# A decoder layer on one Trainium2 core: the router and the end go by token tile, and one unit of expert weights gets a twelfth place

## What is computed

```python
h = rms_norm(x, norm_mix)
z = h @ w_in                                  # queries, keys, values, gates of both branches
oa = moba_attention(qa, ka, va) @ w_oa        # branch A
ob = dsa_attention(qb, kb, vb, ...) @ w_ob    # branch B: indexer, top 64, low-rank keys and values
x = x + (sigmoid(ga) * oa + sigmoid(gb) * ob) @ w_out
x = x + cross_attention(rms_norm(x, norm_x), rms_norm(mem, mem_norm), wq, wk, wv, wo)
# mixture of experts: 4 groups of 8, the best group, in it the best 2 of 8
h = rms_norm(x, norm_moe)
g_logits, e_logits = h @ w_group + b_group, h @ w_router + b_router
weight = max(softmax(g_logits)) * softmax(top2(e_logits in the chosen group))
x = x + sum over the 2 chosen e of weight_e * (silu(h @ w1[e]) * (h @ w3[e])) @ w2[e]
return rms_norm(x, final_norm)
```

## Time and profile before

| | |
|---|---|
| time, median of 3 runs | 702.37 us (700.45 to 703.0) |
| the profiled execution: its own time | 700.77 us |
| its span | 699.0 us |
| mean granted clock | 0.883 |
| PE busy | 514.8 us, 74% |
| DVE busy | 201.8 us, 29% |
| ACT busy | 145.8 us, 21% |
| POOL busy | 15.7 us, 2% |
| DMA moved | 244.21 MB, 349 GB/s on the mean |
| the chain that ended last | PE 51%, DMA 43%, DVE 2%, ACT 2% |

### The profile page before, as it was taken

The page is one execution under the profiler, slowest core; times in us unless marked ns, Lnnn a source line. Parts: engine busy times, 40 slices in busy tenths (PEclk is TensorE's granted clock), DMA queues, the critical chain, the costliest instruction groups (busy, mean ns, idle before and its releaser), DMA issues.

```text
span 699.0 us, 8763 instructions
## 1 busy us (share of the span) xinstructions
PE 514.8 (74%) x3815; PEld 324.6 (46%) x3815; DVE 201.8 (29%) x368; ACT 145.8 (21%) x250; POOL 15.7 (2%) x28
## 2 busy tenths in 40 slices
PE   6999999999999987964735855582475577448284
PEld 5899998989998652411311321140131123114021
DVE  4699565595856430100100000010010000001002
ACT  6555545353644431000000000000000000000002
POOL 1200010001001000000000000000000000000001
PEclk9999999999999998988977797797798779779767
DMA  9899233615689889999999999999999999999991
GB/s 295 251 356 373 101 121 123 240 55 189 217 331 384 348 330 418 432 422 431 427 429 428 428 428 426 429 426 429 427 429 428 426 429 426 429 427 428 418 378 67
DMA packets 48089, 244.21 MB, mean 349 GB/s; under 512 B 8936, under 2 KB 18352, under 8 KB 37296
## 3 DMA queue, kind: packets, MB, share of 16 engines
q1 hardware_dynamic: 48048, 243.62, 86.3%
HBM read 242.53 MB, written 4.22 MB: 353 GB/s over the span
## 4 chain that ended last, share of the span: by engine, by line
PE 51%; DMA 43%; DVE 2%; ACT 2%; issue 1%; SPq 0%; POOL 0%; POOLq 0%; PEldq 0%; DVEq 0%; ACTq 0%
PE ps L640 16%; DMA slots_own<-in_w 13%; DMA slots_late<-in_w 12%; PE ps L934 11%; PE ps L939 7%; PE ps L659 7%; DMA slot_last<-in_w 5%; DMA slot_spare<-in_w 4%; DMA attn_data<-in_w 4%; DMA slot_mixed<-in_w 4%; PE ps L618 2%; PE ps L685 1%; PE ps L761 1%; DMA const<-in_consts 1%; PE ps L948 1%
## 5 line engine op out<-in xcount | busy, mean ns | idle before, releaser
L934 PE MATMUL ps<-slots_late,x_sb 128*32 128x512 f32 x336 | 86.8, 678 | 39.6 <-DMA slot_mixed<-in_w 15.8
L934 PE MATMUL ps<-attn_data,x_sb 128*32 128x512 f32 x176 | 71.5, 698 | 23.2 <-DMA slots_own<-in_w 23.2
L1585 DVE TENSOR_TENSOR bqT<-ps,bqT 128x512 f32<-128x512 f32 x8 | 5.5, 691 | 236.2 <-ACT bqT L1247 236.2
L939 PE MATMUL ps<-slots_own,vb 128*32 128x512 f32 x192 | 54.6, 736 | 24.8 <-DMA slot_last<-in_w 8.6
L410 DVE TENSOR_TENSOR w_low<-slots_own,w_high 128x2048 fp32r<-128x2048 f32 (+1 forms) x32 | 64.8, 2026 | 22.1 <-ACT w_high L1062 22.0
L1244 ACT ACTIVATE vb<-ps 128x256 f32<-128x256 f32 x8 | 3.1, 384 | 309.6 <-PE ps L976 309.6
L934 PE MATMUL ps<-slot_spare,x_sb 128*32 128x512 f32 x112 | 51.9, 668 | 14.1 <-DMA attn_data<-in_w 14.1
L934 PE MATMUL ps<-slots_own,x_sb 128*32 128x512 f32 x240 | 56.2, 674 | 6.9 <-DMA slots_late<-in_w 4.0
L1062 ACT ACTIVATE w_high<-slots_own 128x2048 fp32r<-128x2048 f32 (+1 forms) x32 | 54.3, 1695 | 20.2 <-PE ps L659 10.8
L640 PE MATMUL ps<-h_high,w_high 128*128 128x256 f32 x224 | 55.4, 288 | 0.0
L934 PEld LDWEIGHTS ps<-slots_late,x_sb 128*32 128x32 f32 x336 | 22.0, 123 | 71.0 <-issue 71.0
(11 more groups left out here) (263 smaller groups left out, 930.5 us busy)
## 6 DMA issues: line engine op xcount, KB each, us to landing
slots_own<-in_w SPq DMA_DIRECT2D x27, 2048.0 KB, 33.8
slots_late<-in_w SPq DMA_DIRECT2D x26, 2048.0 KB, 35.2
attn_data<-in_w SPq DMA_DIRECT2D x17, 2048.0 KB, 34.2
slot_last<-in_w SPq DMA_DIRECT2D x9, 2048.0 KB, 36.4
slot_spare<-in_w SPq DMA_DIRECT2D x9, 2048.0 KB, 33.8
slots_own<-in_w_in SPq DMA_DIRECT2D x8, 2048.0 KB, 11.7
slot_mixed<-in_w SPq DMA_DIRECT2D x8, 2048.0 KB, 32.5
slots_own<-in_w_out SPq DMA_DIRECT2D x2, 2048.0 KB, 7.9
```

The source lines that it names most:

```text
L934: return pe.matmul(ps[SLOTS * e:SLOTS * e + SLOTS, 4 + matrix, :], xeT[:, k, SLOTS * e:SLOTS * e + SLOTS], w, start=(k == 0), stop=(k == K ...
L939: return pe.matmul(ps[SLOTS * e:SLOTS * e + SLOTS, 4 + c, :], actT[:, f, SLOTS * e:SLOTS * e + SLOTS], w, start=(f == 0), stop=(f == FC - ...
L1585: dve.tensor_tensor(act_sb, ps[:, 5, :].rearrange("p (q f) -> p f q", f=FC), silu_sb.rearrange("p (f q) -> p f q", f=FC), ALU.mult).then_i ...
```

## The change

It has four parts.

- **A twelfth place.** B's gates `gb`, queries `bqT` and values `vb` become views of one buffer, `slot_extra`, of the size of a place. Unit 3 (`EXTRA_UNIT`) is loaded there, once, issued as the second of all units (`EXTRA_ASKED`), after the last reads of the three tensors. The other units keep the ring of eleven and its order (`ring_place`).
- **Other buffers.** Cross-attention's turned probabilities move from `gb` to `xn`, the router's scratch `rt` from `gb` to `memory_kv_data`, and the final gains from `memory_kv_data` to `slot_extra`; their load now stands after all units on SP.
- **The router.** `route` takes the tokens as the loaded operand and writes 128 x 36 logits straight away. The turning back, with ACT's two copies, is gone. Three of the four `start_sum` matmuls stand ahead of the ranking. DVE makes the places and the first `sel` before it computes the experts' weights (`finish_routing`), and the count goes to bank 7, to be read by the middle of the first gather.
- **The end.** The last sums are done tile by tile; ACT squares tile 0 after its two matmuls and tile 1 after all four. DVE multiplies by scale and gains in one op per half tile (L1625), and SP writes four pieces. The matmul of one element is now only in the branch that is not taken.

```diff
+EXTRA_UNIT = 3
+EXTRA_ASKED = 1
...
+def ring_place(q):
+
+    return q - 1 if q > EXTRA_UNIT else q
...
-        gb = sb("gb", [P, KD, T])
+        slot_extra = sb("slot_extra", [P, SLOT])
+        gb = slot_extra[:, 0:2048].rearrange("p (a b) -> p a b", a=KD)
...
-        bqT = sb("bqT", [P, 4, T])
-        vb = sb("vb", [P, TT, W_HEADS])
+        bqT = slot_extra[:, 2048:3072].rearrange("p (a b) -> p a b", a=4)
+        vb = slot_extra[:, 3072:4096].rearrange("p (a b) -> p a b", a=TT)
...
-        xprobT = flat(gb[:]).rearrange("p (h m t) -> p h m t", h=X_HEADS, m=2)
...
-        fgain = memory_kv_data[:]
+        xprobT = flat(xn[:]).rearrange("p (h m t) -> p h m t", h=X_HEADS, m=2)
+        rt = memory_kv_data[:, 0:14 * TT * EXPERTS].rearrange("p (n t e) -> p n t e", n=14, t=TT)
+        fgain = flat(gb)[:, 0:D]
...
-            for q in range(MOE_RING):
-                s = MOE_SLOTS[q]
+            for i in range(MOE_RING):
+                s = MOE_SLOTS[i]
+                if i == EXTRA_ASKED:
+                    sp.wait_ge(s_done, 8)
+                    sp.wait_ge(o_done, 8)
+                    sp.wait_ge(merge_added, 4)
+                    load_slice(EXTRA_UNIT % 2, 0, EXTRA_UNIT // 2, SLICE, slot_extra, extra_in)
...
+                load(i if i < EXTRA_UNIT else i + 1)
+            for q in range(MOE_RING + 1, ALL_UNITS):
+                i = ring_place(q) - MOE_RING
+                sp.wait_ge(chunk_used, (i if i < EXTRA_UNIT else i + 1) + 1)
                 load(q)
-            job_computed(sp, "xo3")
             sp.dma_start(fgain, final_norm.rearrange("(a d) -> a d", a=1).to_broadcast([P, D])).then_inc(fgain_in, 16)
-            for q in range(MOE_RING, ALL_UNITS):
-                sp.wait_ge(chunk_used, q - MOE_RING + 1)
-                load(q)
...
-                    m = pe.matmul(ps[0:N_RT, 6 + t, 0:P], w_rt[:, k, :], xT[:, k, t * P:(t + 1) * P],
+                    m = pe.matmul(ps[:, 6 + t, P:P + N_RT], xT[:, k, t * P:(t + 1) * P], w_rt[:, k, :],
                                   start=(k == 0), stop=(k == KD - 1))
-                m.then_inc(logitsT_done, 1)
+                m.then_inc(logits_done, 1)
...
+            start_sum(0, 0)
+            start_sum(0, 1)
+            start_sum(1, 0)
...
                 for k in range(KD):
+                    if slices_in and k == 4:
+                        pe.wait_ge(count_read, 1)
...
-                for c in range(2):
-                    pe.wait_ge((y_copied_a, y_copied_v)[c], it + 2)
-                    for t in range(TT):
+                for t in range(TT):
+                    for c in range(2):
+                        pe.wait_ge((y_copied_a, y_copied_v)[c], it + 2)
                         m = pe.matmul(ps[:, 2 * t + c, :], selwT[:, t * P:(t + 1) * P], y_sb[:, 512 * c:512 * c + 512],
                                       start=False, stop=True, skip_group_check=True)
+                    if t == 0 and slices_out:
+                        m.then_inc(top_done, 1)
...
-            act.wait_ge(logitsT_done, 1)
-            act.activation(rlT[:, 0:P], ps[0:N_RT, 6, 0:P], ACT.Copy).then_inc(logitsT_copied, 1)
-            act.wait_ge(logitsT_done, 2)
-            act.activation(rlT[:, P:T], ps[0:N_RT, 7, 0:P], ACT.Copy).then_inc(logitsT_copied, 1)
...
+            for t in range(TT):
+                act.wait_ge((top_done, added)[t], (1, STEPS + 1)[t])
+                square(ps[:, 2 * t:2 * t + 2, :], 5, t, xn[:, t, :].rearrange("p (a b) -> p a b", a=2), fsq)
...
+            for t in range(TT):
+                dve.wait_ge(frstd_set, t + 1)
+                for c in range(2):
+                    dve.scalar_tensor_tensor(xn[:, t, 512 * c:512 * c + 512], ps[:, 2 * t + c, :], rstd[:, 5, t:t + 1],
+                                             fgain[:, 512 * c:512 * c + 512], ALU.mult, ALU.mult).then_inc(out_set[t], 1)
```

128 lines of the change are left out of this document (57 added, 71 removed).

## The result

The changed kernel took **691.65 us** (median of 4 runs, 690.24 to 692.49) where the kernel before took 702.44 beside it (4 runs, 700.45 to 703.0): a ratio of 0.9852, 95% interval 0.9837 to 0.9867. Run again on another occasion it took 691.43 against 701.26, ratio 0.9855 (0.9839 to 0.9872). So it is 10.4 us faster by the ratio; 9.2 were forecast.

The account below looks back on a forecast made before the run. The expert weight stream was taken as the bound, 4.92 us a unit, with TensorE idling before landings. Place 4.9, router 1.8 and tail 2.5 sum to 9.2 us off the 702.37 median: 693.2 us, range 690 to 698.

Parts of the forecast that it names:

- The twelfth place: Early weight stream: unit 3's extra load fills holes, stream one unit ahead for good; gain 4.9 us, bounds 0 and 4.92.
- The router: Routing before the first gather: unit 0 used earlier, so the stream restarts earlier; gain 1.8 us, bounds 0.9 and 2.2.
- This end counts, since DVE's first selection, at 254.07, was released by TensorE's sequencer behind them: Routing: the residual matmuls' end lets DVE's first selection go, near 252.3 instead of 254.07, 1.8 us earlier.
- The 0.9 us of the transposes: Routing: without the two transposes DVE's second logits op starts near 247.15 instead of 248.08, 0.9 us earlier.
- The stream in between: Step 1 onward: the second burst still waits for its landing, 6.7 us earlier, and everything moves with the stream.
- The tail: Behind the last up unit: nothing changes until the sums, then tile-by-tile sums issue the last output earlier; gain 2.5 us.
- Rival D: Tail: TensorE's last bursts change with the clock, 701.4 us at the lower level or 687.3 at the fastest; 5%.
- A: Weight stream: the extra unit delays the rest of the ring, so the place gains nothing; 698.1 us, 6%.
- B: Routing: the selection ends up waiting for ACT or DVE, so the router's gain is not passed on; 695.0 us, 8%.
- C: Router matmuls cost by columns moved, each dropping from 0.24 to 0.12 us; 692.7 us, 5%.
- E: Expert steps: TensorE becomes the bound from a mean clock of 0.55 down, some 730 us at the lower level; 3%.
- F: Whole kernel: the change does nothing, the new load held back and the other gains drowned; 702 us, 2%.

Follow-up runs that it names:

- experiment 7: The kernel before the change, with TensorE's three opening signals given ahead of its wait for the count: 701.6 us, ratio 1.0006.
- experiment 1: The changed kernel without the twelfth place, unit 3 back in the ring of eleven: 696.34 us, ratio 0.9927.
- experiment 2: The changed kernel with unit 3 still in the twelfth place but issued eleventh, at 244 us: 693.42 us, ratio 0.9891.
- experiment 4: The changed kernel with the experts' weights and count computed ahead of DVE's first selection: 691.77 us, run again 690.91 us.
- experiment 3: The changed kernel with everything behind the last down-projection as before the change: 693.97 us, ratio 0.989.
- experiment 6: The changed kernel with logits alone computed the old way, tokens moved, copied by ACT and turned back by TensorE: 692.5 us, ratio 0.9867.

## Why the prediction came out as it did

**Sum and sign were right.** 693.2 us were forecast, the range held the 691.65, and the case was the one that the forecast named. Taken back one at a time, the place, the router and the end cost 4.7 to 5.3, 2.4 and 2.3 to 2.7 us, 9.4 to 10.4 together, against the 10.4 of the whole. No run takes back the other buffers and the later load of the gains; by this sum they are worth 1.0 us or less. Term by term:

*The twelfth place: 4.9 forecast; 4.65 to 4.9 in the chain against the run without it, 4.7 to 5.3 in the time.* Its steps held: the issue at 187.95, SP free again long before unit 1's, the hole at 203 full, the one at 257 still there, the stream no less busy behind it (427 GB/s; 35.3 us from issue to landing). That the front's own weights lose nothing to the new load held too: unit 1's place was asked for at 195.07, which is 1.08 later than in the earlier trace rows, no more than the whole front's shift. Filling holes was the mechanism, and asked late the place gives 2.6 us of it.

*The router: 1.8 forecast, 2.76 measured. This is the term that was mis-sized.* The step that failed is "This end counts, since DVE's first selection, at 254.07, was released by TensorE's sequencer behind them". The row's [0.31 <-PEq L1011] was read as the end of the residual matmuls, 253.89. The sequencer had been waiting for DVE's count, and DVE's own row, places, count, cast, was what ended last; with the signals given early 0.07 us is all that the wait was worth. So what counts for the gain is DVE's chain: the six ops of the weights, 252.01 to 253.22, and the count and the cast left the way to the selection. The prediction knew of that move and gave it no gain, as cover for DVE's lateness. The 0.9 us of the transposes held (0.99). TensorE itself kept to the forecast: counted from the mark its fourth residual matmul ended at 9.4 where 252.15 is 9.5, but the selection had come at 8.5 and not waited for it. The route matmuls cost 0.24 each as before (16 records, eight matmuls, in 1.93 us), not 0.22: the range's other end. That DVE might be late at the gather's first half did not come about: at 254.96 it had waited 0.54 us for TensorE.

*The stream in between: held.* Landing-bound from step 1 on, everything moved together, 6.6 us for 6.7 forecast. (The slices from 16 on have 418 to 432 GB/s in the earlier trace rows, not 417 to 434; nothing hangs on it.) The agreement is partly luck: the two terms together are 7.4 to 7.7, and the later front of this execution took back 1.1. The execution profiled before was 1.6 below its median and the one after is at its own, which is why the medians differ by 10.8 and the profiled executions by 9.1.

*The tail: 2.5 forecast, 2.0 to 2.6 measured in the profiles, 2.3 to 2.7 in the time* (10.6 and 10.2 us from the sums' start to the end, 12.6 with the old end, 12.8 before). The forecast's ops stand as worked out: the last output was issued at 687.2, 7.9 us behind the sums' start, where the forecast had 7.3; the 0.6 between is the sums' lower clock. POOL's op on the sum of squares took 0.19 beside DVE reading PSUM; the 0.55 that the prediction set against its 0.73 is the op behind it (L1629), which takes 0.55 in every profile. That "From the last up unit to the start of the sums (686.21) nothing changes" is true by 0.3 us (23.4 us before, 23.1 now), but for another reason than the prediction had. In the profile of before, two bursts at the lower clock (3.64 and 3.20 us) covered the last landing; in the changed kernel three bursts at full clock end early and TensorE waits 2.4 us for it. The kernel before can do the same: in experiment 7 its last burst waited 2.98 us for `slots_late`. Bursts and landing lie so close together that either ends last. Rival D was priced by bursts alone; on its fast side it has less to give than it says, since the bursts at full clock found the weights not yet there.

*The rivals.* A fell with experiments 1 and 2. B fell: the gain was passed on. C fell too: 0.24 us a matmul at 36 columns moved and 128 loaded, the same as at 128 moved and 36 loaded; by the table of the Trainium skill (TensorE: Matmul & The Clock Gate, Back-to-back issue gap) for a matmul by itself the 36 columns would cost half, which that row does not bear out, and the measurement decides. The same section says that in a stream of loads and matmuls both set the spacing, and with this the row agrees. E: mean granted clock 0.80 between 308 and 656 us, far above the point at which it decides. F fell with the measured time. The output's piece of 256 KB took 2.5 us to landing in the median where 512 KB took 2.6; the estimate by the Trainium skill (DMA: Bandwidth & Descriptors) was 2.6 and 3.2, good for the small piece only. That page gives its fit for the path through GpSimd, while the profile names the queue of this kernel hardware_dynamic.

## What to carry to other kernels

In a kernel that one stream of transfers bounds, an added buffer is worth the empty time that its load can fill, so ask for it where the queue is empty (here at 188 us, 4.65 us gained, and 2.6 when it was asked for at 244). When a wait is put down to a sequencer, look what that sequencer was itself waiting for before pricing the work ahead of it, and on the way to the first use of a ring put only what that use needs: moving the experts' weights behind the first selection brought the restart 1.27 us forward and cost nothing. At the end of a stream, the last transfer's size and the work behind its landing are one sum, and splitting that transfer was worth 1.4 to 2.0 us that no edit on the engines had reached.

## What the runs showed of the hardware

- The granted clock of TensorE falls for some microseconds in one execution of a kernel and not in another. The kernel of experiment 4 ran its first gather in 5.47 us in one profile (clock 0.76 over 252 to 256 us) and in 3.84 in the next; the old end's profile has it at 0.72 over 246 to 252 us. The restart came 1.1 to 1.6 us later with it (16.01 to 16.15 behind the mark for 14.90, 17.78 for 16.17), so a single profile can hide or fake as much of a gain in the front.
- The end's clock went with TensorE's wait for the last unit. The last burst and the sums took 7.0 to 7.3 us in the eight profiles in which that wait was 2.12 to 2.98 us (the changed kernel's two, those of experiments 1, 2, 3, 6, 7 and the old router's), and 5.6 in both of experiment 4, where it was 2.07 and 1.68. That the wait is the cause was not tested by itself.
- The start-up moves with nothing edited in it. TensorE's first matmul waited for the constants until 5.66 us in the profile of before and 6.04 in the one of after, and the transposes behind it (16 records) took 2.06 and 2.77 us: together the 1.1 by which the later profile's front is late. It is not the whole story: without the twelfth place they ended at 11.63 as before, and the mark still stands at 243.62.
- POOL's op on one column takes 0.19 us, and 0.73 beside a DVE op on SBUF alone, seen in all three kernels with the old end.
